# First attention of a two-block transformer kernel: order of transposes, scores and values, and keys converted by Pool

## What is computed

```python
k_c, v_c = mla_kv(ckv_a, ck_pe, kv_norm, w_kvb, None)     # 256 context rows
k_l, v_l = mla_kv(kv_a, k_pe, kv_norm, w_kvb, rope)       # 1024 rows
q_l = mla_q(q_a, q_norm, w_qb, rope)                      # 8 heads of 64 + 32
a_l = blocked_dense_attention(q_l, jnp.concatenate([k_c, k_l], axis=1),
                              jnp.concatenate([v_c, v_l], axis=1), MLA_SCALE)
...
a_c = dense_attention(q_c, k_c, v_c, MLA_SCALE)           # the context attends to itself

def dense_attention(q, k, v, scale):
    s = jnp.einsum('bqhd,bkhd->bhqk', q, k).astype(jnp.float32) * scale
    p = jax.nn.softmax(s, axis=-1).astype(v.dtype)
    return jnp.einsum('bhqk,bkhd->bqhd', p, v)
```

## Time and profile before

| | us |
|---|---|
| median of 3 runs (lowest, highest) | 2911.82 (2911.11, 2916.56) |
| own time of the profiled execution | 2913.63 |
| its span | 2911.8 |
| TensorE products busy | 2611.6 (90%) |
| TensorE weight loads busy | 2106.3 (72%) |
| VectorE busy | 1482.4 (51%) |
| ScalarE busy | 1228.1 (42%) |
| Pool busy | 203.3 (7%) |

### The profile page before, as it was taken

How to read it: one execution, slowest core, us unless ns; L and a number is a source line. 1 busy time by engine, 2 the same in 40 slices (tenths; PEclk the granted TensorE clock), 3 DMA queues, 4 the chain that set the end, 5 groups by cost and what they waited for, 6 DMA issues and landing times. The chain is left out here.

```text
span 2911.8 us, 42158 instructions
## 1 busy us (share of the span) xinstructions
PE 2611.6 (90%) x16327; PEld 2106.3 (72%) x16327; DVE 1482.4 (51%) x2493; ACT 1228.1 (42%) x2303; POOL 203.3 (7%) x293
## 2 busy tenths in 40 slices
PE   5999988988889999999989899999998899986677
PEld 4778976767778989877768688785336777876566
DVE  6122265565555514477775524413775654447752
ACT  6112344444443321266654422214666646224442
POOL 1000010000020000001101000000000100024400
PEclk8999999999999999999999999999999999998889
DMA  7420000000112021100002220101001211120012
GB/s 266 174 103 23 32 17 1 1 1 1 59 58 96 29 65 37 59 2 2 2 1 106 83 87 1 58 29 44 1 1 59 98 44 37 44 73 1 1 44 80
DMA packets 71125, 139.55 MB, mean 48 GB/s; under 512 B 2729, under 2 KB 37954, under 8 KB 70802
## 3 DMA queue, kind: packets, MB, share of 16 engines
q1 hardware_dynamic: 53856, 75.89, 7.7%
q0 software_dynamic: 16832, 60.90, 5.7%
q10 hardware_dynamic: 242, 0.07, 0.0%
HBM read 120.08 MB, written 16.78 MB: 47 GB/s over the span
## 5 line engine op out<-in xcount | busy, mean ns | idle before, releaser
L163 ACT ACTIVATE WORK<-PS 128x512 f32<-128x512 f32 (+5 forms) x307 | 151.4, 493 | 686.7 <-PE PS L790 397.8
L790 PE MATMUL PS<-HT_R,W_R 128*128 128x512 f32 (+1 forms) x864 | 328.7, 380 | 0.0
L163 DVE TENSOR_REDUCE SM<-PS 128x1 f32<-128x1280 f32 (+3 forms) x180 | 199.1, 1106 | 140.3 <-PE PS L1083 96.7
L788 PE MATMUL PS<-WORK_R,W_R 128*128 128x512 f32 (+1 forms) x640 | 245.2, 383 | 28.0 <-issue 17.8
L789 PE MATMUL PS<-WORK_R,W_R 128*128 128x512 f32 (+1 forms) x704 | 266.4, 378 | 0.0
L905 PE MATMUL PS<-WORK_R,HT_R 128*128 128x512 f32 x544 | 217.3, 399 | 22.3 <-DVE W_R L163 21.2
L836 PE MATMUL PS<-BASE,WORK 128*128 128x128 f32 (+1 forms) x1238 | 184.8, 282 | 43.1 <-DVE WORK L163 16.3
L790 PE MATMUL PS<-W_R,WORK_R 128*128 128x256 f32 (+3 forms) x704 | 215.2, 306 | 0.0
L906 PE MATMUL PS<-WORK_R,MIXT_R 128*128 128x512 f32 x544 | 214.3, 394 | 0.0
L907 PE MATMUL PS<-W_R,HT_R 128*128 128x512 f32 x544 | 214.1, 394 | 0.0
L163 ACT ACTIVATE HT<-PS 128x512 f32<-128x512 f32 (+8 forms) x236 | 128.3, 544 | 201.8 <-PE PS L836 118.0
(11 more groups left out here) (284 smaller groups left out, 5688.8 us busy)
## 6 DMA issues: line engine op xcount, KB each, us to landing
MIXT<-in_w_mod POOLq DMA_DIRECT2D x8, 2048.0 KB, 8.6
x_scratch<-WORK POOLq DMA_DIRECT2D x24, 512.0 KB, 2.9
WORK<-x_scratch POOLq DMA_DIRECT2D x24, 512.0 KB, 3.6
W<-in_odd_w_in SPq DMA_DIRECT2D x12, 1024.0 KB, 5.2
W<-in_o_w_in SPq DMA_DIRECT2D x10, 1024.0 KB, 5.2
W<-in_even_w_in SPq DMA_DIRECT2D x5, 2048.0 KB, 8.5
W<-in_w_mod SPq DMA_DIRECT2D x4, 2048.0 KB, 21.6
WORK<-in_x POOLq DMA_DIRECT2D x16, 512.0 KB, 8.1
```

The source lines that it names most:

```text
L163: self.last = Signalled(self, issue(*args, **kwargs))
L788: mm(out, a[0], b_[0], start=k == 0, stop=False)
L790: return mm(out, a[0], b_[1], start=False, stop=k == KT - 1)
```

## The change

1. TensorE's order in step j becomes: first two units of the transposes of j-2; scores of j; third unit of j-2; query work; values of j-2; row sums of j-3. The values wait for the third unit only at their ninth key tile.
2. ScalarE's order: copies of j-2, query copy, exponential of j. VectorE's: copy of the second unit of j-2, maximum of j, query work, product of the values of j-2, reciprocals, product of the row sums of j-3.
3. The loop has two steps less. The query work of a group is done three steps and one step ahead of its first job (two and one around the context tiles).
4. `mla_k` is gone from ScalarE and VectorE. Pool copies and subtracts the keys of heads 4 to 7: the first as soon as job 0 is scored, into a new place (`K_SPARE`), the other three into `KT1R[0..2]` once the jobs 30, 31 and 32 are scored.

```diff
@@ -546,7 +546,7 @@
                 self.bank0 = BANKS - wide * bufs // 512
-                self.steps = len(jobs) + lag + 4
+                self.steps = len(jobs) + lag + 2
                 self.heads = 1 + max(h for _, h in jobs)
@@ -560,16 +560,8 @@
         for m, (_, t) in enumerate(mla_groups[1:], 1):
-            j = first_of[m - 1]
-            if t == 0:
-                steps = (j, j + 2)
-            elif t == 1:
-                steps = (j - 1, j)
-            elif mla_groups[m - 1][1] == 1:
-                steps = (j - 1, j)
-            else:
-                steps = (j, j + 2)
-            for step, what in zip(steps, ("q", "qt")):
+            j = first_of[m]
+            for step, what in zip((j - 2, j - 1) if t == 1 or mla_groups[m - 1][1] == 1 else (j - 3, j - 1), ("q", "qt")):
                 mla_prep.setdefault(step, []).append((what, m))
@@ -652,6 +644,8 @@
         KT1R = HT_R[:, :].rearrange("p (h c) -> p h c", h=MH)
+        K_SPARE = W_R[:, chunk_at["mla_held"] % WS, 1792:3072]
+        SECOND_HIGH = [K_SPARE] + [KT1R[:, i, :] for i in range(3)]
         UT = work(0, 5120).rearrange("p (g c) -> p g c", g=F_G)
@@ -1072,7 +1066,7 @@
                     q = [part[0:M_QK, i, :] for part in QT1[m % 2]]
-                    high = KT1R[0:M_QK, i, :] if hh else K_HIGH[i][0:M_QK, :]
+                    high = (SECOND_HIGH if hh else K_HIGH)[i][0:M_QK, :]
                     low = KT1R[0:M_QK, 4 * hh + i, :]
@@ -1082,19 +1076,20 @@
                 last.then_inc(s_ready, 1)
-                mla_prepare(mla_prep.get(j, []))
...
                 for i in (jj,) if quad else (jj - 1, jj):
-                    for k in range((job_width(i) + 511) // 512):
+                    for k in range(2 if i == jj else 3):
                         landed(pe, ("pt", "mla", i, k))
...
                     for q in range(n):
+                        if q == 8:
+                            landed(pe, ("pt", "mla", jj, 2))
                         for i in range(2):
@@ -1104,10 +1099,11 @@
-            def mla_transposes(jj):
-                pe.wait_ge(p_ready, mla.base + jj + 1)
+            def mla_transposes(jj, ks):
+                if ks[0] == 0:
+                    pe.wait_ge(p_ready, mla.base + jj + 1)
                 n = job_width(jj) // P
-                for k, q in enumerate(range(0, n, 4)):
+                for k, q in list(enumerate(range(0, n, 4)))[ks[0]:ks[-1] + 1]:
                     transposes(("pt", "mla", jj, k), [mla.P[jj % 2][:, (q + r) * P:(q + r + 1) * P] for r in range(min(4, n - q))],
@@ -1123,15 +1119,17 @@
             for j in range(mla.steps):
+                jj = j - mla.lag - 1
+                if 0 <= jj < J:
+                    mla_transposes(jj, (0, 1))
                 if j < J:
                     mla_scores(j)
-                jj = j - mla.lag - 2
+                if 0 <= jj < J:
+                    mla_transposes(jj, (2,))
+                mla_prepare(mla_prep.get(j, []))
                 if 0 <= jj < J:
                     mla_values(jj)
-                jj = j - mla.lag - 1
-                if 0 <= jj < J:
-                    mla_transposes(jj)
-                jj = j - mla.lag - 3
+                jj = j - mla.lag - 2
                 if 0 <= jj < J:
@@ -1752,16 +1750,6 @@
-            def mla_k(i):
-
-                if i == 0:
-                    for a in (2, 3):
-                        for c0, _ in TG:
-                            landed(act, ("kt", a, c0))
-                    act.wait_ge(k_rope_all, 10)
-                act.wait_ge(s_ready, mla.base + half_jobs - 4 + i + 1)
-                f(KT1R[0:M_QK, i, :], KT1[0:M_QK, 4 + i, :], ACT.Copy).then_inc(k_high, 1)
-
             for t in range(NT):
@@ -1769,28 +1757,25 @@
             for j in range(mla.steps):
-                jj = j - mla.lag
-                if 0 <= jj < J:
-                    if jj >= 2:
-                        pe_read(act, ("pt", "mla", jj - 2, (job_width(jj - 2) - 1) // 512))
-                    from_dve()
-                    cols = CTX if mla_jobs[jj][3] else COLS
-                    for i in range(job_width(jj) // cols):
-                        c = slice(i * cols, (i + 1) * cols)
-                        ins = f(mla.P[jj % 2][:, c], score_at(mla, jj)[:, c], ACT.Exp, bias=neg_of(jj)[:, i:i + 1], scale=M_SCALE,
-                                accum_out=sums_of(jj)[:, i:i + 1])
-                    ins.then_inc(p_ready, 1)
-                for what, m in mla_prep.get(j, []):
-                    if what == "qt":
-                        mla_qt(m)
-                if half_jobs - 3 <= j <= half_jobs:
-                    mla_k(j - half_jobs + 3)
                 jj = j - mla.lag - 1
...
                             copy_unit(("pt", "mla", jj, k), mla.PT[jj % 2][:, c:c + m], m)
+                for what, m in mla_prep.get(j, []):
+                    if what == "qt":
+                        mla_qt(m)
+                if j < J:
+                    if j >= 2:
+                        pe_read(act, ("pt", "mla", j - 2, (job_width(j - 2) - 1) // 512))
+                    from_dve()
+                    cols = CTX if mla_jobs[j][3] else COLS
+                    for i in range(job_width(j) // cols):
+                        c = slice(i * cols, (i + 1) * cols)
+                        ins = f(mla.P[j % 2][:, c], score_at(mla, j)[:, c], ACT.Exp, bias=neg_of(j)[:, i:i + 1], scale=M_SCALE,
+                                accum_out=sums_of(j)[:, i:i + 1])
+                    ins.then_inc(p_ready, 1)
             late = boundary(1)
@@ -2419,10 +2404,6 @@
-            def mla_k(i):
-                dve.wait_ge(k_high, i + 1)
-                v.tensor_tensor(KT1R[0:M_QK, 4 + i, :], KT1[0:M_QK, 4 + i, :], KT1R[0:M_QK, i, :], ALU.subtract).then_inc(k_low, 1)
-
             def mla_prepare(steps):
@@ -2435,6 +2416,10 @@
             for j in range(mla.steps):
+                jj = j - mla.lag - 1
+                if 0 <= jj < J:
+                    n = min(512, job_width(jj) - 512)
+                    copy_unit(("pt", "mla", jj, 1), mla.PT[jj % 2][:, 512:512 + n], n)
                 if j < J:
@@ -2459,13 +2441,7 @@
                         v.tensor_copy(heads4(mla.RX[m % 2]), RECIP[:, 0:4].unsqueeze(2).to_broadcast([P, 4, 64])).then_inc(recip_ready, 1)
-                jj = j - mla.lag - 1
-                if 0 <= jj < J:
-                    for k, c in enumerate(range(0, job_width(jj), 512)):
-                        if k % 2 == 1:
-                            n = min(512, job_width(jj) - c)
-                            copy_unit(("pt", "mla", jj, k), mla.PT[jj % 2][:, c:c + n], n)
-                jj = j - mla.lag - 3
+                jj = j - mla.lag - 2
                 if 0 <= jj < J and jj == last_of[mla_jobs[jj][0]]:
@@ -2915,6 +2891,15 @@
                 copy(KT1R[64:96, h, :], KT1R[64:96, 0, :]).then_inc(k_rope_all, 1)
+
+            for a in (2, 3):
+                for c0, _ in TG:
+                    landed(pool, ("kt", a, c0))
+            for i in range(4):
+                pool.wait_ge(s_ready, mla.base + (half_jobs - 4 + i if i else 1))
+                copy(SECOND_HIGH[i][0:M_QK, :], KT1[0:M_QK, 4 + i, :]).then_inc(k_high, 1)
+                pool.wait_ge(k_high, i + 1)
+                nc.gpsimd.tensor_tensor(KT1R[0:M_QK, 4 + i, :], KT1[0:M_QK, 4 + i, :], SECOND_HIGH[i][0:M_QK, :], ALU.subtract).then_inc(k_low, 1)
```

## The result

The changed kernel takes 2898.02 us, the median of four runs (2894.19 to 2901.31); the kernel before, measured beside it, 2913.8 (2911.11 to 2916.56). The ratio is 0.9945, with a 95% interval of 0.9928 to 0.9963. The profiled execution took 2901.31 with a span of 2899.5, so between profiled executions the change is 12.3 us of either. First the head of the page after: the span and the busy times.

A forecast was written before the change was run, and what follows sets the result against it. In the first attention's loop no engine is full; TensorE, 87% busy, has gaps that can be won, mostly waits for ScalarE evictions. Order +1.2, keys -4.2 and clock -4.6 sum to -7.6, forecasting 2904.3 us, range 2896 to 2916.

The forecast's parts named there:

- the forecast's own 2900 to 2909: Whole kernel: range around the forecast time of 2904.3 us, given a chance of 0.45.
- rival A: Loop's clock: drops at 500 and 424 go too, -3.3, giving 2901, or 2899.8 with the order costing nothing; chance 0.18.
- The keys, -4.2: Chain of four jobs around 600: the conversion leaves ScalarE and VectorE, saving 4.2 us; first head taken as 0.
- Pool's price, 4.4 a head between 2.5 and 5.7: Keys on Pool: copy 1.25 plus 2.5 x 1.27 is 4.4 us a head; 2.5 from below, 5.7 with doubled copy.
- The order's plain round, +0.32 each: Plain rounds: 22.28 us laid out against 22.0 for the old order, +4.2 over 13 rounds.
- The four waits: TensorE's waits in a plain round: 0.27, 1.12, 0.55 and 1.13 us; a fifth, before the second value product, 0.26.
- The loop's ends: First six jobs +1.3 us; second pair of four-head jobs and last, broken round -1.2; drain -3.1.
- The clock, -4.6: Loop's clock: three of five drops, at 616, 708 and 722, go, at 1.55 us each.
- The drop at 500: Plain round of the loop: this clock drop was to stay, its stretch without products being 3.1, now 3.0 us.
- B: Between scores C and D, 2.96 us without products: clock drops in most rounds, ten more give 2921; chance 0.12.
- C: Chain maximum, exponential, copy exceeds its 5.93: 0.3 us more at two waits in 16 rounds, +9.6, 2914; chance 0.15.
- D: Keys' conversion not hidden, by Pool and VectorE excluding each other or Pool late: 4.2 not won, 2910; chance 0.10.

The follow-up runs named there:

- keys alone: The kernel before with only the keys' conversion given to Pool, old order kept; 2905.84 us, ratio 0.9971 to the kernel before.
- the repeat: The changed kernel run once more, unchanged; 2899.28 us, ratio 0.9950 to the kernel before.
- Order alone: The changed kernel with the keys converted on ScalarE and VectorE again, new order kept; 2906.2 us, ratio 0.9974 to the kernel before.
- seven profiles of the new order: Profiles of the changed kernel, its repeat, order alone, slow Pool, copy first, VectorE's row-sums product first, and both moves together; 2877.46 us for both moves.
- whole transposes: The changed kernel with all three units of transposes ahead of the scores; 3021.19 us, ratio 1.0354 to the kernel before.
- the copy first: The changed kernel with ScalarE's first-unit copy of every second job ahead of the next job's exponential; 2886.76 us, ratio 0.9915 to the kernel before.
- slow Pool: The changed kernel with each copy of a head's keys on Pool made four times; 2905.62 us, ratio 0.9974 to the kernel before.

## Why it came out so, point by point

The direction was right and 2898.0 lies within the range of 2896 to 2916, but the sum was too small: -7.6 against -12.3 between profiled executions. 2898.0 is also below the forecast's own 2900 to 2909; it lies where rival A stood, which had a chance of 0.18. More than half of the gain is the clock's, and the old order doesn't always have the five drops of that profile (keys alone had two), so the hit is in part luck.

- **The keys, -4.2.** The eight jobs from 30 took 50.13 before with a drop in them, 48.46 in the third profile of the same kernel without one, and 44.46 after: **-4.0** without the drop. The first head was taken as 0. It holds VectorE at the loop's start (below): the first six jobs took 33.66 in the profile after, where it did so, and 32.78 in the repeat, where it didn't, each with one drop, so it cost **+0.9** in the first. The two scores that answer to the earlier trace rows, 28.01 apart before, are 22.31 apart:

```profile
593.13 0.54 PEld L1073 LDWEIGHTS PS<-WORK_R 96*128 96x128 f32 x3
...
615.44 0.54 PEld L1073 LDWEIGHTS PS<-HT_R,WORK_R 96*128 96x128 f32 x3
```

- **Pool's price, 4.4 a head between 2.5 and 5.7.** It is 1.25 and 2.93, 4.2 from one head's start to the next's. The copy was at the lower bound, and the two-input operation took 2.93 where 2.5 x 1.27 = 3.2 had been put.
- **The order's plain round, +0.32 each.** This step failed. The four waits came out as laid out, to 0.06 us, and the fifth to 0.09. The round is 22.14 where 22.28 was laid out, and the round before is 22.10 where 21.96 was laid out. Both errors are 0.14, of opposite sign, and the difference of the two layouts carries both: +4.2 was predicted and 13 x 0.04 = +0.5 came. I had the measured 22.10 in hand and put the layout against a layout, in the belief that common errors cancel; they did not.
- **The loop's ends.** The drain was to be shorter by 3.1 and is by 3.2 (from the last scores to SyncE's row 16.39 before, 13.17 after). The first six jobs were to cost 1.3: with one drop near 425 in both, they take 32.78 in the repeat of the changed kernel and 31.58 before, +1.2. The second pair of four-head jobs and the last, broken round were to give 1.2: the sixteen jobs around the pair take 0.2 more at full clock (98.4 less two drops of 1.7 before, 95.2 with none after), and the step from job 66 to 67 is 4.7 where it was 5.8, together -0.9. So all of these held, and the order is +0.5 + 1.2 - 0.9 - 3.2 = **-2.4** at full clock, where +1.2 was predicted. Order alone bears it out: from its first scores to the loop's end it takes 391.66 with one drop, the kernel before 400.94 with five, and without the drops that is 2.5 less.
- **The clock, -4.6.** Five drops became one, not two: 8.5 us lost became 1.7, **-6.8**. Three drops were priced at 1.55 and were to go; four went, at 1.7 each. That fewer and shorter stretches without products bring fewer drops fits all seven profiles of the new order, and whole transposes shows the reverse. But the argument for single places was weak. I gave each drop its local cause, and the two repeats of the kernel before show that places change with the code unchanged. Even the number isn't the order's alone: with the old order it was five, six and five, and two in keys alone. The drop at 500, "to stay", went.
- **Together:** -2.4 - 4.0 + 0.9 - 6.8 = -12.3 against -12.5 measured from the first scores (423.21 before, 423.56 after) to the loop's end.
- **Rivals.** A, the clock gets better still, is what came, as to its drop at 500 and its "order costs nothing"; a drop at the start stayed. B's mechanism is real (whole transposes), and the change is on the safe side of it. C, a chain longer than its rows, fell: 1.18 and 1.12. D fell: three of Pool's heads are hidden at twice their time. The part of it that exists is VectorE held by Pool, below.
- **What was to show it.** The round, the waits, four pairs on Pool of 4.2 us and 22.3 over the four jobs around 600 came as said; the drops of the clock are one where two were said.

## What to carry to other kernels

When the order of a hand-made schedule changes, lay out the new one from measured durations, but compare it with the measured round, and treat the layout's own error on the old order as the size of what can't be predicted. An instruction that an in-order engine holds behind an unrelated wait (here a 0.60 copy behind a 1.33 exponential that itself waits for a maximum) is worth looking for first: moving that one copy gave 1.07 us a round and some 9 to 12 us in all, by ratios or by medians, where the whole change gave 15; and moving a second instruction paid only once the first had moved. Repeat the profile of the kernel before, if drops of the clock carry a term of the sum: here their places changed with the code unchanged, and one order lost from 3.4 to 11.9 us to them.

## What the runs showed of the hardware

**VectorE held by Pool.** The addition that ends a query's rotation has two inputs in SBUF and takes 0.29. Where it met a subtraction of Pool's, it was held. Pool's and then VectorE's timeline in the changed kernel:

```profile
597.64 2.92 POOL L2902 TENSOR_TENSOR HT_R<-HT,HT_R 96x1280 fp32r<-96x1280 f32 x1
```

```profile
598.88 0.81 DVE L163 TENSOR_TENSOR WORK<-PS,TABL 128x128 f32<-128x128 f32 x3
599.72 0.99 DVE L163 TENSOR_TENSOR WORK<-WORK 128x128 f32<-128x128 f32 x1
```

The same two with the copy first:

```profile
591.90 2.90 POOL L2907 TENSOR_TENSOR HT_R<-HT,HT_R 96x1280 fp32r<-96x1280 f32 x1
```

```profile
592.07 0.81 DVE L163 TENSOR_TENSOR WORK<-PS,TABL 128x128 f32<-128x128 f32 x3
592.91 2.05 DVE L163 TENSOR_TENSOR WORK<-WORK 128x128 f32<-128x128 f32 x1
```

It ends 0.15 to 0.16 after Pool's instruction ends (600.71 against 600.56, 594.96 against 594.80), while the three operations ahead of it, with one input in the accumulation memory, ran beside Pool at their usual 0.81. The round was 22.31 in place of 22.14 in the changed kernel, and 22.30 in place of 21.07 with the copy first. Held by 0.70 and 1.76, the rounds are 0.17 and 1.23 longer, so 0.53 of it was slack both times. In slow Pool the addition was held by only 0.43 (it took 0.72), within that slack, and the round stayed 22.14. The prediction had the trace show only that Pool is slowed; now it shows VectorE waiting. The Trainium skill (SBUF — State Buffer, "SBUF: two separate sides") says that of a Pool operation and a VectorE operation with two SBUF inputs the later is blocked for the whole instruction of the earlier; the trace agrees, with 0.99 and 2.05 for 0.29. It isn't only the addition. In slow Pool a scaling of 128 x 4 with one input was held (1.49 for 0.17), and in keys alone a copy of `SM` into `W` (1.92 for 0.29), while the scaling of 128 x 1 kept its 0.15 to 0.16 beside Pool each time. In the changed kernel's first profile the addition was also held at the loop's start, behind the first head (1.27 at 428.54), which is the 0.9 above.

**The clock moves between executions of one kernel**, as told above: five, six and five drops in the loop in three profiles of the kernel before, at partly different places, at 1.7 us each and twice that for two of them.
